# Projecting the indexer's queries for tokens 256 to 1087 only, in two chunks of 416 columns

## The reference, cut to what matters

```python
p = jnp.einsum('btd,dp->btp', h, w)          # h: tokens x 2048
qa, ka, va, qi, wi, ki, za, qb, kb, vb, zb, ga, gb = jnp.split(p, _OFFS, axis=-1)
...
allowed = (s_pos[None, :] // CHUNK) <= (t_pos[:, None] // CHUNK)     # CHUNK = 64
dots = jnp.einsum('bthd,bsd->bths', qi, ki) * (D_IDX ** -0.5)
score = jnp.einsum('bths,bth->bts', jax.nn.relu(dots), wi) * (H_IDX ** -0.5)
score = jnp.where(allowed[None], score, NEG)
_, idx = lax.top_k(score, n_sel)             # n_sel = 256
```

## Time and profile before

| | |
|---|---|
| median of 3 runs | 3430.92 us |
| fastest, slowest | 3427.84, 3432.37 us |
| profiled execution: span from first to last instruction | 3430.3 us |
| instructions | 48118 |
| PE busy | 3196.8 us, 93% of the span |
| DVE, POOL, ACT busy | 1325.4, 882.6, 852.5 us |
| mean granted TensorE clock | 0.968 |

### The profile page before, as it was taken

How to read it: one execution, slowest core, us unless ns; L and a number is a source line. 1 busy time by engine, 2 the same in 40 slices (tenths; PEclk the granted TensorE clock), 3 DMA queues, 4 the chain that set the end, 5 groups by cost and what they waited for, 6 DMA issues and landing times. The chain is left out here.

```text
span 3430.3 us, 48118 instructions
## 1 busy us (share of the span) xinstructions
PE 3196.8 (93%) x18207; PEld 3024.1 (88%) x18221; DVE 1325.4 (39%) x2169; ACT 852.5 (25%) x1761; POOL 882.6 (26%) x652
## 2 busy tenths in 40 slices
PE   5999999999999999999999996975777999989997
PEld 5999999999999999999999995764567999978875
DVE  5000543537264650497000006754994112120411
ACT  4111121222221211311111114543553111031422
POOL 1222212121212122122122113422552222133453
PEclk7999999999999999999999997986998999999999
DMA  4223223222223222122542214233424333262442
GB/s 143 68 74 82 73 63 79 60 78 65 75 60 84 57 78 79 54 65 74 96 111 79 83 59 117 64 93 78 78 54 147 121 104 121 67 227 92 151 155 99
DMA packets 356873, 309.53 MB, mean 90 GB/s; under 512 B 34745, under 2 KB 316441, under 8 KB 353225
## 3 DMA queue, kind: packets, MB, share of 16 engines
q1 hardware_dynamic: 328384, 244.02, 25.4%
q10 hardware_dynamic: 28360, 63.76, 6.6%
HBM read 232.31 MB, written 75.48 MB: 90 GB/s over the span
## 5 line engine op out<-in xcount | busy, mean ns | idle before, releaser
L587 PE MATMUL banks<-h_hi,w_in_tile_hi 128*128 128x384 f32 (+1 forms) x3792 | 838.4, 329 | 10.0 <-POOL w_in_tile_lo L458 7.5
L587 PE MATMUL banks<-h_lo,w_in_tile_hi 128*128 128x384 f32 (+1 forms) x3792 | 837.0, 328 | 0.0
L587 PE MATMUL banks<-h_hi,w_in_tile_lo 128*128 128x384 f32 (+1 forms) x3792 | 836.1, 328 | 0.0
L458 POOL TENSOR_TENSOR w_in_tile_lo<-w_in_tile_raw,w_in_tile_hi 128x512 fp32r<-128x512 f32 x312 | 407.5, 1307 | 1587.5 <-ACT w_in_tile_hi L478 1587.5
L587 PEld LDWEIGHTS banks<-h_hi,w_in_tile_hi 128*128 128x128 f32 (+1 forms) x3792 | 650.6, 187 | 22.8 <-POOL w_in_tile_lo L458 8.1
L587 PEld LDWEIGHTS banks<-h_hi,w_in_tile_lo 128*128 128x128 f32 (+1 forms) x3792 | 648.7, 187 | 0.9
L587 PEld LDWEIGHTS banks<-h_lo,w_in_tile_hi 128*128 128x128 f32 (+1 forms) x3792 | 646.0, 187 | 1.0
L478 ACT CAST w_in_tile_hi<-w_in_tile_raw 128x512 fp32r<-128x512 f32 x312 | 192.9, 620 | 1391.3 <-PE banks L587 1300.0
L754 DVE MAX8 top<-score 128x8 f32<-128x384 f32 (+6 forms) x224 | 247.2, 1103 | 33.0 <-DVE score L757 1.1
L757 DVE MATCH_REPLACE8 score<-top,score 128x384 f32<-128x384 f32 (+6 forms) x224 | 242.9, 1085 | 0.0
L2095 PE MATMUL banks<-w_out_tile_hi,m_hi 128*128 128x512 f32 x576 | 227.1, 394 | 15.7 <-DVE m_lo L2025 13.4
(11 more groups left out here) (243 smaller groups left out, 3531.0 us busy)
## 6 DMA issues: line engine op xcount, KB each, us to landing
w_in_tile_raw<-in_w_in SPq DMA_DIRECT2D x312, 256.0 KB, 2.9
product<-spill ACTq DMA_DIRECT2D x78, 544.0 KB, 3.4
w_out_tile_raw<-in_w_out SPq DMA_DIRECT2D x128, 256.0 KB, 3.1
u_b<-product SPq DMA_DIRECT2D x32, 544.0 KB, 6.3
merged<-u_b ACTq DMA_DIRECT2D x16, 544.0 KB, 7.3
x_rows<-in_x_prompt SPq DMA_DIRECT2D x8, 1024.0 KB, 5.1
b_q_raw<-product SPq DMA_DIRECT2D x16, 512.0 KB, 7.8
w_br_tile_raw<-in_w_br_b SPq DMA_DIRECT2D x64, 128.0 KB, 2.9
```

Source lines behind the costliest of these rows:

```text
L458: pool.tensor_tensor(s.w_lo[:, q, :, :], s.w_raw[:, q, :, :], s.w_hi[:, q, :, :].bitcast(F32), ALU.subtract).then_inc(lo_made, 1)
L587: last = pe.matmul(ps[0:m, 3 * slot + c, 0:w], w_[:, q, kq, 0:m], h_[:, k, t0:t0 + w], start=(k == 0 and w_ is s.w_hi and h_ is s.h_hi), s ...
```

## The change

The eight tiles of the indexer's queries are projected in two chunks of 416 columns, tokens 256 to 671 and 672 to 1087, evacuated in the same two chunks, and stored from token 256 on. `chunks_of` chooses the chunks by the tile's column in `w_in`; all other tiles keep `TCH`. The plan, the loads of weights and all waits are as before.

```diff
 TCH = ((0, 384), (384, 384), (768, 320))
+ALL_SELECTED = TOPK
+TCH_I = ((ALL_SELECTED, 416), (ALL_SELECTED + 416, 416))
...
+    def chunks_of(col):
+
+        return TCH_I if QI <= col < WI else TCH
...
-            def evacuate(n, slot, kind, rows, n_half, row0, m=P):
+            def evacuate(n, slot, kind, rows, n_half, row0, m=P, chunks=TCH):
...
-                for c, (t0, w) in enumerate(TCH):
+                for c, (t0, w) in enumerate(chunks):
...
-                act.dma_start(rows(row0), spill[0:m, slot, :]).then_inc(spilled[slot], 16)
+                t0 = chunks[0][0]
+                act.dma_start(rows(row0)[:, t0:T], spill[0:m, slot, t0:T]).then_inc(spilled[slot], 16)
...
-                                 None if before is None else i + before, at + col)
+                                 None if before is None else i + before, at + col, chunks=chunks_of(col))
...
-            def product(n, slot, m=P, wait_acc=True, wait_split=True, scored=None):
+            def product(n, slot, m=P, wait_acc=True, wait_split=True, scored=None, chunks=TCH):
...
-                            for c, (t0, w) in enumerate(TCH):
+                            for c, (t0, w) in enumerate(chunks):
...
-                                scored=None if scored is None else (scored, j, count))
+                                scored=None if scored is None else (scored, j, count), chunks=chunks_of(col))
```

## The result

The changed kernel takes 3378.25 us (median of 4 runs, 3375.01 to 3379.5) where the kernel before, on the same chip, takes 3430.09 us: a ratio of 0.9846, 95% interval 0.9833 to 0.986. The direction came out, and so did the time saved in the stage; the gain is 51.8 us where the sum said 47.6, and 52.6 us in the five more rounds. The profiled execution spans 3375.6 us, 54.7 us less than that of before.

The account below looks back on a forecast made before the run. The prediction took PE alone to bound the eight query tiles; 5.94 us saved a tile made 47.6 us, and 3430.9 - 47.6 = 3383.3 us as a median. The range was 3378 to 3388 us, with 0.93 on the forecast.

Parts of the forecast that it names:

- the sum: Whole kernel: eight tiles save 47.6 us, so 3430.9 us becomes 3383.3 us as a median, 1.4% faster.
- The bound of the stage: Tiles 1 to 8, the indexer's queries: bound by PE alone, busy 192.60 of 192.60 us at clock 1.00.
- The term of the sum: Tiles 1 to 8: 188.1 ns a matmul of 416 columns, 18.06 us a tile instead of 24.00, 5.94 us saved each.
- the line between two widths: PE's matmul cost: straight line from 362.7 columns at 166.7 ns to 512 at 226.7 ns, 0.4018 ns a column.
- Weighing the page against the rows: Tiles 1 to 8: the skill page's 518 cycles for 512 columns would give 41.9 us; trace rows contradict it and were preferred.
- The edits costed at nothing: Tiles 1 to 8: changed evacuation, smaller store and faster weight pipeline stay hidden behind PE and cost 0 us.
- Rounding up to 512: Rival, tiles 1 to 8: 416 columns charged like 512, 21.76 us a tile, gain 17.9 us, 3413 us; chance 0.03.
- weights that can't follow: Rival, tiles 1 to 8: weight loads landing singly make a tile 19.6 us, gain 35 us, 3396 us; chance 0.02.
- a saving given back: Rival, after tile 8: PE later waits for scores or masks, so no change, 3431 us; chance 0.01.
- a slower clock in the stage: Rival, tiles 1 to 8: granted clock falls to 1.2 GHz, eight tiles take 266 us, 3505 us; chance 0.01.
- That a chunk's cost depends on the chunks beside it: Tiles 1 to 8: named, without a size, as a dependence beyond a chunk's own width that would make the prediction wrong.
- What is late next: Everything after tile 8: no chain bypasses the eight tiles, so the saving arrives whole; lower-clock stretches may fall differently.

Follow-up runs that it names:

- five more rounds: The changed kernel run again with no edit: 3377.03 us (5 runs) against 3429.62 us for the kernel before, ratio 0.9845.
- 288-288-256: The changed kernel with the same 832 columns in three chunks (288, 288, 256) instead of two of 416: 3384.51 us, ratio 0.9867.
- 512-320: The changed kernel with the same 832 columns in chunks of 512 and 320 instead of 416 twice: 3377.23 us, ratio 0.9847.
- 416-416-256: The changed kernel with TensorE projecting all 1088 tokens in chunks of 416, 416 and 256, evacuation and store as changed: 3432.58 us, ratio 1.0009.
- the padding kernels: 128 or 256 instructions of tiny unread transposes added on TensorE early: changed kernel 3379.91 and 3376.4 us, kernel before 3424.31 and 3429.94 us.
- the padded kernel before (256): The kernel before with 128 tiny unread transposes, 256 instructions, added on TensorE while it idles early: 3429.94 us, ratio 1.0004.

## Why the prediction was right and where it was wrong

Taken as a whole the prediction was wrong: the time came out 4.8 us under the 3383.0 us, at the very edge of the range, for a reason that it had put at nothing. Its steps one by one:

**The bound of the stage** was right: PE alone, without a wait, at clock 1.00, before and after.

**The term of the sum** was right: 188.1 ns a matmul forecast on the line between two widths, 187.8 measured; 47.6 us for eight tiles, 47.8 measured. That it fits to 0.3 ns is in part luck. One end of the line was a mixed set, and the experiments show that unlike widths side by side cost more than like ones (512 and 320 against 416 twice: 380.0 against 375.6 ns a set). Drawn on to the 277.3 columns that a matmul has on average in 288-288-256, the same line gives 132.4 ns, and 127.8 ns were measured.

**Weighing the page against the rows** was right: 41.9 us, an estimate from the Trainium skill, page "TensorE: Matmul & The Clock Gate", section "Back-to-back issue gap", against 47.8 measured. On this kernel 416 columns take 187.8 ns, 14.4 ns over the columns, where that section's table leaves some 6 cycles, 2.5 ns. The section gives that table for an isolated matmul; here every matmul has a weight load of its own, so the two needn't agree.

**The edits costed at nothing** were right: evacuation and store gave nothing when made alone, and tiles 9 and 10 and the scores kept their lengths.

**The rivals.** Rounding up to 512, weights that can't follow, a saving given back and a slower clock in the stage are each excluded by the 18.03 us tiles and the unchanged stretches behind them. That a chunk's cost depends on the chunks beside it, named as what could make the prediction wrong, is true, but worth only 0.2 to 0.3 us a tile in the two kernels that show it (512-320 and 416-416-256).

**The step that failed** is in "What is late next": that with every chain going through the eight tiles, the saving arrives whole and only shifts what follows, apart from stretches at the lower clock whose differences the three runs hold already. The profiled executions differ by 7.6 us behind the projections, 4.8 of it in the merge, and over more rounds the medians still differ by 4.8 us more than the stage gives. The change took 384 instructions out of TensorE's program text, one and a half packets of 16 KB at the 256 instructions a packet that the padding kernels bear out, and so moved every later fetch against the work. In the kernel before one falls among the issues of a weight load that PE then waits for: the load's first quarter lands late, PE stops 3.4 us, and 6.8 us behind the stop run at 1.2 GHz. The sum had no term for this. Moved by 128 instructions in the kernel before, the fetch is worth 5.0 us, and 2.9 to 3.5 us in the changed kernel: about 1% of the merge and a tenth of the gain.

Two smaller faults. I read 0.625 ns a column out of ACT's 480 and 439 ns; 41 ns for 64 columns are 0.64 ns, and the 500 ns for 416 columns stay. And I set the profiled execution's span of 3430.3 us beside the median of 3430.9 us. Each run of this study is 1.8 us longer than its span (3377.38 against 3375.6 us), so the profiled execution of before was a run of some 3432.1 us, near the top of its three (3432.37 us).

**What stays open.** How a fetch delays other transfers (6.1 to 6.4 us to landing against 4.9 to 5.3 us) and lengthens issues (3.65 against 2.58 us for four) isn't shown, only that both come with the fetch and go when it is moved. That the late quarter is what makes the merge longer, by PE's stop and the clock behind it, is read from the traces; no run changes the landing alone, and moving these loads ahead of the fetch gave 3.7 us, not all of it. The changed kernel gains 2.2 us by the same move without a fetch near it. That these packets are TensorE's own follows from their moving with instructions added to TensorE alone. That one holds 256 of them fits too: the queue has 85 packets in the kernel before and 84 in the changed one, and 256 added instructions make them 86 and 85. The 2.2 us by which the output phase differs between the two profiled executions (418.7 and 416.5 us) was not traced to a cause, nor why the padded kernel before (256) has a stop of only 1.7 us, and so a merge of 408.6 us, at the median of the kernel before.

## What to carry to other kernels

Where one engine is busy without a gap, price the edit by that engine's start-to-start distance in two widths and draw the line between them; it held here to 0.3 ns a matmul between its ends, and missed by 4.6 ns outside them. An edit that changes how many instructions stand in an engine's program also moves its instruction fetches against all later work, and here, in a short prologue whose loads come just in time, that was worth 3 to 5 us. Before a few tenths of a per cent are put down to an edit, pad the program by half a fetch and by a whole one, and look at whether the difference stays.

## What the runs showed of the hardware that I had not expected

- Instruction fetches as a resource: 16 KB packets, 256 of TensorE's instructions each; 128 instructions more moved one from 26 to 12 us into the merge and made the kernel 5.0 us faster. Two transfers of 128 KB issued within some 1.5 us of such a fetch landed in 6.1 to 6.4 us, and in 4.9 to 5.3 us without one.
- What a matmul costs over its columns, at one column a cycle of 2.4 GHz, depends on the widths side by side (mean of a set): 12.2 ns for 288, 288, 256; 13.3 ns for 512 alone; 14.4 ns for 416 alone; 15.6 ns for 384, 384, 320; 16.7 ns for 512, 320; 17.8 ns for 416, 416, 256.
